# The w1 weights of a mixture of experts arrive in four 2 MB pieces instead of eight 1 MB pieces

## What is computed

```python
def moe_ffn(xt, router_w, router_b, w1, b1, w2, b2):     # xt: 512 x 1024
    top_val, top_idx = lax.top_k(xt @ router_w + router_b, 4)
    gates = softmax(top_val)
    ...
    def expert_block(args):
        xb, e = args
        hcat = xb @ w1[e] + b1[e]                        # w1[e]: 1024 x 2048
        h_glu, h_lin = split(hcat, 2)
        h_glu = minimum(h_glu, 7.0); h_lin = clip(h_lin, -7.0, 7.0)
        act = h_glu * sigmoid(1.702 * h_glu) * (h_lin + 1.0)
        return act @ w2[e] + b2[e]                       # w2[e]: 1024 x 1024
```

## Time and profile before

| | us |
|---|---|
| median of 3 runs | 1683.49 |
| lowest and highest | 1683.31, 1687.91 |
| the profiled execution | 1683.98 |
| its span, first to last instruction | 1682.2 |
| TensorE matmuls busy | 1598.8 (95%) |
| VectorE busy | 644.8 (38%) |
| GpSimd busy | 416.6 (25%) |
| ScalarE busy | 398.4 (24%) |
| share of the DMA engines, queue of SyncE | 70.6% |
| w1 products (L1305), 6144 instructions | 672.9 |
| w2 products (L1354), 6144 instructions | 344.0 |

### The profile page before, as it was taken

How to read it: one execution, slowest core, us unless ns; L and a number is a source line. 1 busy time by engine, 2 the same in 40 slices (tenths; PEclk the granted TensorE clock), 3 DMA queues, 4 the chain that set the end, 5 groups by cost and what they waited for, 6 DMA issues and landing times.

```text
span 1682.2 us, 38327 instructions
## 1 busy us (share of the span) xinstructions
PE 1598.8 (95%) x16168; PEld 925.6 (55%) x16168; DVE 644.8 (38%) x1203; ACT 398.4 (24%) x604; POOL 416.6 (25%) x464
## 2 busy tenths in 40 slices
PE   5999999997999999999999999999999999999990
PEld 5999987785788954334434433433443443443340
DVE  3799786213315343223224223223322322322336
ACT  4332123454312241112111112111211111111211
POOL 5343333353243342111111211211111121121122
PEclk8999999999999889999999999999999999999995
DMA  6223223221065539999999999999999999999956
GB/s 181 76 78 98 76 76 100 75 76 50 27 239 212 170 134 408 402 409 411 397 406 408 397 408 411 401 403 409 408 397 410 409 395 407 410 401 407 408 232 254
DMA packets 123085, 482.63 MB, mean 287 GB/s; under 512 B 17105, under 2 KB 66425, under 8 KB 73156
## 3 DMA queue, kind: packets, MB, share of 16 engines
q1 hardware_dynamic: 114020, 464.98, 70.6%
q0 software_dynamic: 8880, 16.54, 3.1%
q10 hardware_dynamic: 144, 0.52, 0.1%
HBM read 474.22 MB, written 16.86 MB: 292 GB/s over the span
## 4 chain that ended last, share of the span: by engine, by line
PE 92%; DVE 4%; ACT 2%; issue 1%; DMA 1%; POOL 0%; SPq 0%; ACTq 0%; POOLq 0%; DVEq 0%
PE banks L1305 39%; PE banks L939 27%; PE banks L1354 20%; PE banks L1291 2%; DVE h_res L1708 1%; PE banks L1255 1%; PE banks L1269 1%; DMA x_sb<-in_x_dram 1%; DMA y_in<-y_rows 0%; PE banks L1325 0%; PE banks L1152 0%; PE banks L1154 0%; ACT bias_parts L891 0%; PE banks L1133 0%; DVE meta_sb L1392 0%
## 5 line engine op out<-in xcount | busy, mean ns | idle before, releaser
L1305 PE MATMUL banks<-w_ring,xT 128*32 128x512 f32 x6144 | 672.9, 593 | 4.0 <-ACT row_pick L898 2.9
L1305 PEld LDWEIGHTS banks<-w_ring,xT 128*32 128x32 f32 x6144 | 199.6, 110 | 434.9 <-issue 426.3
L1354 PE MATMUL banks<-w_ring,actT 128*32 128x256 f32 x6144 | 344.0, 380 | 0.0
L1354 PEld LDWEIGHTS banks<-w_ring,actT 128*32 128x32 f32 x6144 | 196.6, 110 | 143.5 <-issue 19.1
L1675 DVE TENSOR_TENSOR hid<-banks,bias 128x512 f32<-128x512 f32 x96 | 63.9, 665 | 484.1 <-PE banks L1305 484.1
L554 POOL TENSOR_TENSOR w_lo<-stage,w_hi 128x2048 fp32r<-128x2048 f32 x38 | 175.0, 4606 | 289.9 <-ACT w_hi L690 289.9
L939 PE MATMUL banks<-u_hi,w_hi 128*128 128x264 f32 (+1 forms) x544 | 182.8, 336 | 4.1 <-ACT gates L792 2.1
L939 PE MATMUL banks<-u_hi,w_lo 128*128 128x264 f32 (+1 forms) x544 | 181.4, 333 | 0.0
L939 PE MATMUL banks<-u_lo,w_hi 128*128 128x264 f32 (+1 forms) x544 | 180.7, 332 | 0.0
L910 ACT ACTIVATE bias<-banks 128x512 f32<-128x512 f32 x32 | 19.1, 597 | 560.6 <-PE banks L1325 560.6
L1462 DVE SCALAR_TENSOR_TENSOR banks<-conv_in,taps,banks 128x512 f32<-128x512 f32 x224 | 150.8, 746 | 0.0
(11 more groups left out here) (251 smaller groups left out, 1648.2 us busy)
## 6 DMA issues: line engine op xcount, KB each, us to landing
w_ring<-in_expert_w_dram SPq DMA_DIRECT2D x384, 1024.0 KB, 15.1
stage<-in_w_in_dram SPq DMA_DIRECT2D x20, 1024.0 KB, 5.2
stage<-in_w_in_dram SPq DMA_DIRECT2D x16, 512.0 KB, 5.3
y_in<-y_rows SPq DMA_DIRECT2D x3, 2048.0 KB, 12.3
stage<-in_conv_pw_w_dram SPq DMA_DIRECT2D x4, 1024.0 KB, 5.3
stage<-in_mlstm_out_w_dram SPq DMA_DIRECT2D x4, 1024.0 KB, 5.2
stage<-in_w_out_dram SPq DMA_DIRECT2D x4, 1024.0 KB, 5.3
x_sb<-in_x_dram SPq DMA_DIRECT2D x4, 512.0 KB, 6.8
```

What stands on the lines that cost most here:

```text
L1305: last = nc.tensor.matmul(banks[32 * g:32 * (g + 1), t].rearrange("p (c j) -> p c j", j=64), xT[:, k, 32 * t:32 * (t + 1)], units, start=k ...
L1354: last = nc.tensor.matmul(banks[32 * g:32 * (g + 1), 3 + t, 0:GRP], actT[:, t, k], w2_ring[k // 2][:, k % 2, GRP * g:GRP * (g + 1)], start ...
```

## The change

The eight places of w1 become four double places of the same size in the same bytes of SBUF. `load_chunk` is called for even c only and moves 2 MB: rows 128c to 128c + 255, rows 2p and 2p + 1 of them to partition p, 16 KB in one run. A double place has one semaphore for its arrival, `ring_in[c]`, and one for its release, `ring_used[c]`, with c even, which TensorE increments after the odd chunk. The release of the last pair is `hid_mm`, as it was for the last chunk. Chunk k of the contraction is now every second column of a block of 256, and the token side is dealt out likewise. w2 is as before.

```diff
-        w1_ring = [at(f"w1_ring{c}", [P, 2, DFF], F32, ring_end - chunk * (c + 1)) for c in range(W1C)]
+        w1_pair = [at(f"w1_pair{j}", [P, 2, 2, DFF], F32, ring_end - 2 * chunk * (j + 1)) for j in range(W1C // 2)]
...
                 if c < W1C:
-                    src = expert_w1[0, bass.ds(e, 1), P * c:P * (c + 1), :].rearrange("e p (g n) -> p (e g) n", g=2)
-                    sp.dma_start(w1_ring[c], src).then_inc(ring_in[c], 16)
+                    assert c % 2 == 0
+                    src = expert_w1[0, bass.ds(e, 1), P * c:P * (c + 2), :].rearrange("e (p r) n -> p (e r n)", p=P)
+                    sp.dma_start(w1_pair[c // 2].rearrange("p r h n -> p (r h n)"), src).then_inc(ring_in[c], 16)
...
-            for c in range(4):
+            for c in range(0, 4, 2):
                 load_chunk(0, c)
...
-            for c in range(4, 6):
-                load_chunk(0, c)
+            load_chunk(0, 4)
...
-            for c in range(6, RING):
+            for c in [6] + list(range(W1C, RING)):
                 load_chunk(0, c)
...
-                for c in range(RING):
+                for c in list(range(0, W1C, 2)) + list(range(W1C, RING)):
-                    if c in (W1C - 1, RING - 1):
+                    if c in (W1C - 2, RING - 1):
...
-                    col = P * (4 * m + k)
-                    last = nc.tensor.matmul(banks[:, X_BANKS[m], SLOTS * k:SLOTS * (k + 1)], u2[:, i, col:col + P], in_slot[:, i],
+                    col = 2 * P * (2 * m + k // 2) + k % 2
+                    last = nc.tensor.matmul(banks[:, X_BANKS[m], SLOTS * k:SLOTS * (k + 1)], u2[:, i, col:col + 2 * P - 1:2], in_slot[:, i],
...
-                    last = nc.tensor.transpose(banks[:, k // 4, SLOTS * (k % 4):SLOTS * (k % 4 + 1)], xs[:, P * k:P * (k + 1)],
+                    last = nc.tensor.transpose(banks[:, k // 4, SLOTS * (k % 4):SLOTS * (k % 4 + 1)], xs[:, 2 * P * (k // 2) + k % 2:2 * P * (k // 2 + 1):2],
...
-                            units = w1_ring[k].rearrange("p h (c g j) -> p g (h c) j", g=CG, j=64)[:, g]
+                            units = w1_pair[k // 2][:, k % 2].rearrange("p h (c g j) -> p g (h c) j", g=CG, j=64)[:, g]
...
-                        pe.wait_ge(ring_in[k], (n + 1) * 16)
+                        if k % 2 == 0:
+                            pe.wait_ge(ring_in[k], (n + 1) * 16)
...
-                        last.then_inc(ring_used[k], 1)
+                        if k % 2:
+                            last.then_inc(ring_used[k - 1], 1)
...
-                    for k in range(KT - LATE, KT):
-                        pe.wait_ge(ring_in[k], (n + 1) * 16)
+                    pe.wait_ge(ring_in[KT - 2], (n + 1) * 16)
...
-                            if t == TG - 1 and k < KT - 1:
-                                last.then_inc(ring_used[k], 1)
+                            if t == TG - 1 and k % 2 and k < KT - 1:
+                                last.then_inc(ring_used[k - 1], 1)
```

## The result

The changed kernel takes 1695.15 us (median of 4 runs, 1693.31 to 1695.91) where the kernel before takes 1684.20 in the same runs: a ratio of 1.0059, with a 95% interval of 1.0045 to 1.0074. It is 11 us slower, and lies above the forecast range of 1681.2 to 1692. The profiled execution took 1695.91 us around a span of 1694.2.

What follows compares the result with a forecast made beforehand. The prediction took TensorE's own work, 32.24 us an expert, to bound the kernel, with the weight stream 3.5 us in hand at the end. Its terms, 0 + 0 + 0 + 0, gave 1683.5 us, range 1681.2 to 1692.

Steps and rivals of the forecast that it cites:

- the first part (waits and issues): TensorE waits for 4 w1 semaphores an expert, not 8, and SyncE issues 8 DMAs, not 12: taken at 0.
- The second part: Release by pairs in the w1 ring: even chunks issued later, one-time lag of 0 to 2 us, 0 on TensorE.
- The third part: w1 runs of 16 KB: stream needs 19.6 us an expert for 19.9, 0.28 us less; nothing on TensorE's path.
- the prediction's signs: Signs of being right: chain stays 32.24 us, loads 140 ns, last w1 pair lands within 17 us in the last experts.
- The fourth part: Transposes and first tokens' products read every second column, a step of 8 bytes: 0 to 27 us, taken at 0.
- the high end: Stepped weight loads at factor 1.49, 68 ns more for a transpose: 17.5 us in the experts, 27 us in all.
- VectorE's row: VectorE's act_v product, output hopping 128 bytes, takes 632 ns where the add of the same shape takes 425, factor 1.49.
- A: Stepped weight load of the transposes is slow: 9 us gives 1692, the whole high end 1710; chance 0.10.
- B: Weight stream becomes the bound at the wait for c = 6 and 7: 1718, or 1690 at a quarter; chance 0.07.
- C: GpSimd's y stores land later behind larger packets, row_now's copy still covered: 1683.5; within the 0.80 for unchanged time.
- D: w1 transfer is cut at 8 KB as before, only releases change: 1683.5 or 1684; within the 0.80 for unchanged time.
- E: Something after the experts or in the stage before gets shorter by SyncE's lighter queue; chance 0.03.

Runs made afterwards that it cites:

- experiment 8: Kernel before with releases by pairs alone (1 MB transfers, eight arrivals, no step): 1697.57 us beside 1697.29, ratio 1.0001.
- experiment 2: Changed kernel without the step, VectorE writing u2 with even columns first so transposes read neighbouring columns: 1684.66 us, ratio 1.0004 to the kernel before.
- Experiment 10: Changed kernel without the step (u2 written even columns first), half of the third group's w2 products left out: 1678.25 us, ratio 0.9959 to the kernel before.
- 9: Kernel before with half of the third group's w2 products left out: 1676.63 us, ratio 0.9950.
- experiments 3 and 4: Kernel before with w1 rows and token columns dealt out at steps of 4 and 8: 1695.38 us beside 1684.49, and 1706.49 us beside 1697.29.
- experiments 5 and 6: Kernel before, then changed kernel, with the eight transposes made as ordinary fp32 products with the unit matrix: 1731.67 and 1738.52 us, beside 1697.29.
- experiment 11: Kernel before with releases by pairs alone (1 MB transfers, no step), half of the third group's w2 products left out: 1676.14 us, ratio 0.9951.

## Why the prediction was wrong, step by step

**What bounds the kernel, and the first part (waits and issues), were right.** TensorE's own chain set the end before and after, all pieces but the transposes kept their length to 0.01 us, and half the waits and issues gave nothing that shows.

**The second part was right for the time and too small for the lag.** Releases by pairs cost nothing (experiment 8, and 2 against the kernel before). In experiment 2 the last pair's lag in the second expert was 2.7 us higher, where I had allowed 0 to 2. The margin took it, with nothing to spare at the end.

**The third part failed in its size.** It took 427 GB/s from the load of y_in and set 0.28 us an expert as the gain of the stream. Experiment 10 against 9 shows 32.51 for 32.43 us, no gain, and in experiment 2 the lag grew by 0.30 us an expert or more. The load of y_in ran with nothing of GpSimd's beside it; the weights share the engines with its gathers and scatters. Whether that is the reason was not tried. The last pair of the changed kernel landed within 17 us to the end, as the prediction's signs had it, but that was luck: TensorE's expert had grown to 32.56 us, about the stream's own time. The miss cost no time, since nobody waits for the stream there.

**The fourth part is the step that failed.** It set the cost of the stepped read between 0 and 27 us and took 0. The loads take 77 ns more, above the high end's 68, but the eight overlap in part, so that 0.32 us of the chain of each expert is lost and not 0.55: 10.2 us for the 17.5 of the high end. "A step of 8 bytes is far nearer to 4 than to 128" was the wrong measure of nearness. The loss is there in full as soon as neighbours are no longer read, and does not grow with the step (experiments 3 and 4). The reason by overlap was half right: it takes 37 of the 77 ns away (0.32 / 8 = 0.040 us are left), not all. The 9.3 us for the first tokens were too high, since ordinary fp32 products pay 5 ns (experiments 5 and 6). The mean of 296 ns which they were worked out from mixed two clocks: the loads of L1255 took 187 to 337 ns before and 193 to 337 after, the short ones at a granted clock of 1.00 and the long ones at 0.50, so the group says nothing on a step as it stood.

The rule that I quoted from the Trainium skill (SBUF — State Buffer, Door 1: the DMA port swizzle), that two hits on a 16-byte line keep full bandwidth, does not hold for this load. Two hits on a line (step 2) cost 77 ns more, and one hit (step 4) costs 83. VectorE's row gave the better price. For the ordinary fp32 product it nearly holds: a step of 2 costs 5 ns there.

**The rivals.** A is what happened, at the price of 10 us, which the prediction had named as a third of the high end (1692); its chance of 0.10 was too low for an operation of which no row existed and which stands on the chain with nothing to hide it, and the range ended at the weak form of it. B did not happen in the changed kernel, but the margin that it rests on is as thin as the prediction had it: without the step it was used up in the last experts. (11.5 us over 31 experts are 0.37 us and not 0.38, so 0.11 us more would have decided, not 0.12.) C was right in both halves: with 2 MB transfers GpSimd's stores land 2 to 3 us later (experiments 2 and 10), and the row copy is still covered; in the changed kernel itself it waited 172.2 us in all for 164.8. D's premise is refuted: the packets fell from 123085 to 104652. For E there was nothing.

Experiment 2 is the change without its loss. It equals the kernel before, and does not beat it: the stream gained nothing, and TensorE's own chain was the bound up to the last experts.

## What to carry to other kernels

A layout of the contraction that suits the DMA transfer has to be matched by the other operand of the product, and that is where this one was paid for. Look for the instruction that has to read or write with a step, and deal the data out where it costs little, here in VectorE's write of u2, four instructions for the whole kernel instead of eight loads an expert. Where an operation on the chain of every iteration has no row in the trace, don't settle its cost by analogy at the cheap end: 40 ns times 256 is 10 us. And a stream that nobody waits for may already be slower than the compute and live on its head start, here 32.4 to 32.5 us for 32.24. The growth of issue-to-landing times shows it, and it caps what any saving on the compute side can bring (56 us less work gave 8).

## What the runs showed of the hardware that I had not expected

- The weight load of an fp32 transpose (96x128) takes 140 ns from neighbouring columns and 207 to 223 ns at a step of 2, 4 or 8 columns; that of an ordinary fp32 product takes 191 and 196. In a block of eight, a transpose costs 101 or 141 ns of the chain.
- One transpose over the full array between products on column groups of 32 costs 0.37 us of the chain, against 0.10 us in a block.
- With 2 MB transfers in SyncE's queue GpSimd's indirect stores land 9.2 us (experiment 2) or 10.3 us (experiment 10) after their issue, with 1 MB transfers 7.2 to 7.3 us (before, experiment 11).
- The same kernel before took 1684.49 us beside some experiments and 1697.29 beside others. In the profiles of the latter most of TensorE's weight loads for the w1 products follow one another where four of them lie over one another in the former, and w1's first block takes 12.97 us for 12.87 (experiment 8). The cause is open.
